# Retention and windowed-attention trunk on one core: the fifth piece's low part made by VectorE, block 0's closing norm ahead of the first rotation

## What is computed

```python
h = h + retention_layer(rmsnorm(h, ret_norm), ret_w_in, ret_w_out)
kb, vb = shared_kv(h, kv_norm, w_kv)
h = h + swa_sink_layer(rmsnorm(h, swa_norm), swa_w_in, swa_sinks, swa_w_out, kb, vb)
return rmsnorm(h, final_norm)

def retention_layer(h, w_in, w_out):
    q, k, v, g = split(h @ w_in)          # per head: q, k of 256, v, g of 512
    q, k = apply_rope(q), apply_rope(k)
    o = normalized((q k^T * decay) v + q R)    # R: the carried state
    return (o * silu(g)) @ w_out
```

## Time and profile before

| | us |
|---|---|
| median of 3 runs | 2452.99 (2448.79 to 2453.55) |
| profiled execution | 2453.43 |
| its span, first to last instruction | 2451.6 |
| block 1's heads, about | 645 to 1086 |
| TensorE busy | 2403.7 |
| VectorE busy | 1456.6 |
| ScalarE busy | 666.2 |
| GpSimd busy | 425.3 |

### The profile page before, as it was taken

How to read it: one execution, slowest core, us unless ns; L and a number is a source line. 1 busy time by engine, 2 the same in 40 slices (tenths; PEclk the granted TensorE clock), 3 DMA queues, 4 the chain that set the end, 5 groups by cost and what they waited for, 6 DMA issues and landing times.

```text
span 2451.6 us, 28645 instructions
## 1 busy us (share of the span) xinstructions
PE 2403.7 (98%) x11264; PEld 1975.1 (81%) x11264; DVE 1456.6 (59%) x2014; ACT 666.2 (27%) x1450; POOL 425.3 (17%) x310
## 2 busy tenths in 40 slices
PE   7999999999999999999999999999999999999998
PEld 6888888877778787888888888888888887888886
DVE  6554655577664655653858564655566745647384
ACT  2312312235220211122532221222352212313243
POOL 2111111221254645530010000000001100001000
PEclk9999999999999999999999999999999999999999
DMA  8667575654898888974369877775357977786433
GB/s 351 268 236 291 195 267 214 249 189 181 322 386 325 328 327 292 339 263 181 117 221 326 275 258 261 272 255 192 144 178 241 332 262 264 251 282 248 172 103 146
DMA packets 126393, 613.25 MB, mean 250 GB/s; under 512 B 8544, under 2 KB 9312, under 8 KB 104288
## 3 DMA queue, kind: packets, MB, share of 16 engines
q1 hardware_dynamic: 117424, 575.94, 65.4%
q10 hardware_dynamic: 8880, 36.18, 3.9%
HBM read 459.00 MB, written 153.09 MB: 250 GB/s over the span
## 4 chain that ended last, share of the span: by engine, by line
PE 90%; DVE 7%; issue 1%; ACT 1%; DMA 0%; POOL 0%; DVEq 0%; SPq 0%; POOLq 0%; ACTq 0%
PE ps L693 29%; PE ps L695 28%; PE ps L694 28%; PE ps L1146 2%; DVE ff L2105 1%; PE ps L1156 1%; DVE ff L1992 1%; PE ps L954 1%; DVE fr L1575 1%; PE ps L841 1%; DVE mx L2145 1%; DVE xlo L1575 0%; DVE ff L2175 0%; DMA raw<-in_stream 0%; PE ps L1086 0%
## 5 line engine op out<-in xcount | busy, mean ns | idle before, releaser
L693 PE MATMUL ps<-whl,xhi 128*128 128x512 f32 (+1 forms) x1088 | 416.8, 383 | 3.7 <-DVE xlo L1575 2.2
L695 PE MATMUL ps<-whl,xlo 128*128 128x512 f32 (+1 forms) x1088 | 411.6, 378 | 0.0
L694 PE MATMUL ps<-whl,xhi 128*128 128x512 f32 (+1 forms) x1088 | 410.5, 377 | 0.0
L693 PE MATMUL ps<-xhi,whl 128*128 128x512 f32 x768 | 303.8, 396 | 17.7 <-DVE xlo L1579 16.3
L695 PE MATMUL ps<-xhi,whl 128*128 128x512 f32 x768 | 300.4, 391 | 0.0
L694 PE MATMUL ps<-xlo,whl 128*128 128x512 f32 x768 | 299.8, 390 | 0.0
L693 PE MATMUL ps<-whl,fr 128*128 128x512 f32 x704 | 283.3, 402 | 2.3 <-DVE whl L1617 2.1
L695 PE MATMUL ps<-whl,fr 128*128 128x512 f32 x704 | 279.9, 398 | 0.0
L694 PE MATMUL ps<-whl,fr 128*128 128x512 f32 x704 | 279.6, 397 | 0.0
L693 PEld LDWEIGHTS ps<-whl,xhi 128*128 128x128 f32 x1088 | 204.9, 188 | 42.1 <-issue 3.1
L695 PEld LDWEIGHTS ps<-whl,xlo 128*128 128x128 f32 x1088 | 204.7, 188 | 38.7
(11 more groups left out here) (199 smaller groups left out, 3725.1 us busy)
## 6 DMA issues: line engine op xcount, KB each, us to landing
whl<-split_w SPq DMA_DIRECT2D x68, 2048.0 KB, 8.5
whl<-split_w SPq DMA_DIRECT2D x110, 1024.0 KB, 6.8
split_w<-whl SPq DMA_DIRECT2D x44, 2048.0 KB, 7.2
whl<-vg_w SPq DMA_DIRECT2D x64, 1024.0 KB, 6.8
raw<-in_stream SPq DMA_DIRECT2D x44, 1024.0 KB, 9.4
vg_w<-ff SPq DMA_DIRECT2D x32, 1024.0 KB, 8.8
raw<-in_stream SPq DMA_DIRECT2D x50, 512.0 KB, 9.7
whl<-comb_w SPq DMA_DIRECT2D x24, 1024.0 KB, 6.2
```

The lines of the kernel that those rows point to most:

```text
L693: pe.matmul(dst, lhs[0], rhs[0], start=start, stop=False)
L694: pe.matmul(dst, lhs[0], rhs[1], start=False, stop=False)
L695: return pe.matmul(dst, lhs[1], rhs[0], start=False, stop=stop)
```

## The change

The low part of piece 4 is taken from GpSimd (L647 falls, and `own_lo` with it) and given to VectorE as `comb_less_hi(4)`, between the output additions (0, 1) and (0, 2). That of piece 5, which stood after the addition (1, 1), comes after (1, 2). In head 0 of block 1 the closing norm of block 0 comes ahead of the first rotation; the wait for it before `comb_less_hi(0)` stays.

```diff
--- before.py
+++ after.py
@@ -625,7 +625,7 @@
                 if c == Q0:
                     h_root(Place("post", 0), 1)
             h_root(Place("post", 0), 2)
-            def comb_piece(at, j, own_lo=False):
+            def comb_piece(at, j):
 
                 pool.wait_ge(comb_raw[j % 2].sem, at(comb_raw[j % 2], 2 * (j // 2) + 2))
                 b11, b21, b12, b22 = [raw[j % 2][:, i * 512:(i + 1) * 512] for i in range(4)]
@@ -641,10 +641,6 @@
                     pool.wait_ge(comb_hi_stored.sem, Place("head", at.b, at.h - 1)(comb_hi_stored, PIECES))
                     pool.wait_ge(comb_lo_stored.sem, Place("head", at.b, at.h - 1)(comb_lo_stored, PIECES))
                 pool.tensor_scalar(stage[:, 0, :].bitcast(F32R), raw[j % 2], 1.0, 1.0, ALU.mult, ALU.mult).then_inc(comb_hi.sem, 1)
-                if own_lo:
-                    pool.wait_ge(comb_hi.sem, at(comb_hi, j + 1))
-                    pool.wait_ge(comb_lo_stored.sem, at(comb_lo_stored, j))
-                    pool.tensor_tensor(stage[:, 1, :].bitcast(F32R), raw[j % 2], stage[:, 0, :], ALU.subtract).then_inc(comb_lo.sem, 1)
 
             def x_sums_lo(b):
 
@@ -669,7 +665,7 @@
                         x_sums_lo(b)
                     o_root(at)
                     if b < FAST:
-                        comb_piece(at, 4, True)
+                        comb_piece(at, 4)
                         comb_piece(at, 5)
                     else:
                         y_sums_lo(at)
@@ -1897,6 +1893,8 @@
                         dve.tensor_tensor(dst[:, 0, :], rot[:, 0, :], sinp[:, 1, :], ALU.subtract).then_inc(rope_rot.sem, 1)
                         dve.tensor_tensor(dst[:, 1, :], rot[:, 1, :], sinp[:, 0, :], ALU.add).then_inc(rope_rot.sem, 1)
 
+                    if seam:
+                        final_norm(b - 1)
                     dve.wait_ge(ropes_scaled.sem, at(ropes_scaled, 0))
                     dve.wait_ge(w_used.sem, at(w_used, 1))
                     rope(0, rot)
@@ -1907,7 +1905,6 @@
                         split_chunk(n0 + 2)
                     if combine:
                         if seam:
-                            final_norm(b - 1)
                             dve.wait_ge(fin.sem, Place("post", b - 1)(fin, TT))
                         comb_less_hi(0)
                     dve.wait_ge(q_lo.sem, at(q_lo, 1))
@@ -2022,13 +2019,15 @@
                     if first:
                         split_chunk(n0 + 7)
                     add_to_h(0, 1)
+                    if combine:
+                        comb_less_hi(4)
                     add_to_h(0, 2)
                     add_to_h(0, 3)
                     if first:
                         split_chunk(n0 + 8)
                     for t in range(TT):
                         add_to_h(1, t)
-                        if combine and t == 1:
+                        if combine and t == 2:
                             comb_less_hi(5)
 
                 if first:
```

## The result

| | before | after |
|---|---|---|
| median of 20 runs, us | 2451.51 | 2455.20 |
| lowest to highest | 2445.97 to 2453.78 | 2453.22 to 2457.36 |
| profiled execution | 2453.43 | 2454.64 |
| its span | 2451.6 | 2452.8 |

The ratio is 1.0016 with a 95% interval of 1.0010 to 1.0022: the change makes the kernel 3.7 us slower, little, but clear of the noise. The forecast was 1.3 us faster, so it missed by 5.0 us and had the sign wrong. The new median lies inside the stated range, and the change of 3.7 us is under the 4.9 us (0.2%) that the chances went by; the direction is what was wrong. The lines of `kernel.py` are 3 or 4 lower than before for most of VectorE and TensorE, and L647 is no more.

What follows compares the result with a forecast made beforehand. TensorE, busy 98% of the span, was taken as the bound. Gains of 9.3 + 3.1 + 1.6 = 14.0 us less 12.7 us of cost left 1.3 us off the 2452.99 median: 2451.7 us, range 2442.5 to 2457.

Steps and rivals of the forecast that it cites:

- Part 1: Block 1, fourth gate product: without L647 on GpSimd, TensorE's waits there go; 9.3 us, plus 3.1 us of half clock.
- The four waits: TensorE's transposes waiting on the gate product in block 1: 8.6 us in all, longest 2.6, forecast to go whole.
- The half clock in the gain: TensorE's half-speed stretches behind the transposes' waits in heads 0 and 2 of block 1 would go: 3.1 us gained.
- The half clock in the cost: Half-speed TensorE behind two of three new waits at the starts of heads 1 to 3: 3.1 us lost.
- The three waits: TensorE waiting for the first chunk at the starts of heads 1, 2 and 3: 3.2 us each, 9.6 us lost.
- the two rows: Earlier store-to-chunk landings, mid-head 17.6 us and head's end corrected to 15.2; the forecast took 16.4 between.
- Part 2: Start of head 0, block 1: the closing norm moves into VectorE's idle time, ending TensorE's wait for the second rotation; 1.6 us gained.
- The sum: Whole kernel: 14.0 us gained less 12.7 us of cost, a net gain of 1.3 us.
- D: Head starts: slower queue, chunk 4.9 us late three times, half clock each time; 5.4 us slower, 2458.4; chance 0.12.
- B: Head starts: queue catches up in 15.1 us, chunk 1.9 us late, clock full; gain 8.3 us, 2444.7; chance 0.20.
- C: Head starts: only bytes count, group takes 13.9 us, chunk 0.7 us late; gain 11.9 us, 2441.1; chance 0.06.

Runs made afterwards that it cites:

- experiment 5: Kernel before with the closing norm moved and GpSimd's low part of piece 4 held until the fourth gate product is done: 2446.85 us, ratio 0.9987.
- experiment 8: Kernel before, unchanged, run once more for its spread and a second trace: 2450.20 us, ratio 1.0001 to before.
- experiment 1: Kernel before with only the closing norm moved ahead of the first rotation: 2449.66 us, ratio 0.9996.
- experiment 2: The change without the moved norm: 2457.22 us, ratio 1.0029 to the kernel before.
- experiment 9: The change with piece 4's low part one output addition later, behind the third: 2464.31 us, ratio 1.0056 to the kernel before.
- experiment 10: The change without the moved norm, with piece 4's low part right behind the fourth gate product: 2441.97 us, ratio 0.9964 to before.
- experiment 3: The change with VectorE making piece 4's low part right behind the fourth gate product: 2440.71 us, ratio 0.9959 to before.
- experiment 6: The change with only the load of the next head's raw piece 0 issued behind its first chunk: 2440.27 us, ratio 0.9958 to before.

## Why the prediction was wrong, point by point

- **Part 1, L647 off GpSimd: right.** The four waits are gone, the gate product takes 0.69 us, no wait took its place there. Experiment 5 showed the mechanism with GpSimd still doing the work.
- **The half clock in the gain: the largest part of the miss.** The sum booked 3.1 us for two stretches, because the one profiled execution had two. That execution was 1.9 us over the median of 20 runs; a second one had none (experiment 8). The median of three that the forecast went by was 1.5 us over that of 20 as well. The typical gain was 1 to 2 us smaller than booked, and the forecast laid the whole 14.0 on a median.
- **The half clock in the cost: mis-sized, and this turned the sign.** "I count two of three": all three waits had it, 4.8 us for 3.1. With that alone the cost is 14.4 us, over the gain of 14.0. The 2.6 us with and 1.9 us without were taken for a bound between two cases, but of the 15 waits of 1.7 to 2.8 us in four traces (before, experiments 1, 5 and 8) six brought it, one of 2.0 us among them, and nine did not, one of 2.8 us among them; all nine waits of 3.0 us and more, in the traces of the change and of experiments 2 and 9, brought it.
- **The three waits, the mechanism: right, in place, order and number.** The size: 3.2 us forecast, 3.5 measured (3.6, 3.5, 3.4 from start to start), 10.6 us for 9.6. The low part took 2.85, 2.28, 2.62 us in heads 0 to 2, for 2.9. From store to landing it was 16.6, 17.1 and 16.6 us for 16.4, so the average of the two rows was nearer than either of them (15.2 and 17.6). The store went out 13.0 to 13.6 us ahead of the head's end, for 13.2.
- **Part 2, the norm: right in the trace.** It was doubled to 8.9 us by GpSimd's L635 as allowed for, stayed hidden, and the wait of 1.5 us is gone. What it is worth in time stays open (experiment 10).
- **The sum.** 14.0 less 12.7 was a difference of two large terms, each uncertain by a few us. Measured against the first trace it is 14.0 less 15.4; against the median of before it is 12.1 less 15.4, 3.3 us slower. The 5.0 us of the miss are, by the traces: 1.0 of waits, 1.7 of the third stretch, 1.9 that the profiled execution of before was over the median of its 20 runs, and 0.6 that the one of after was under its own; together 5.2, since the account gives 1.4 where the spans differ by 1.2. That four waits would go and three come was right. Even against the execution that the sum was worked out from the change is a loss, for the cost's two terms; the gain's half clock made it a larger one.
- **The rivals.** D named the mechanism that won, the late chunk with half clock each time, and set its turning point at a delay of "3.1 with the clock lost each time". The measured delay was 3.5, past that point. B and C (a queue that catches up) were wrong: 16.6 to 17.1 us, not 15.1 or 13.9.

## What to carry to other kernels

When a wait is taken off the engine that sets the time, look at what used that wait as slack: here the DMA queue had 20.7 to 22.3 us for a group that takes about 19, and a version that takes the wait away has to give the queue room again, by an earlier store or another order of issue. Where the result of a moved operation is stored, follow that store through its queue to the next load that somebody waits for, and price it with the time from first issue to last landing of such a group elsewhere in the trace. And subtract no term that one profile shows and a second may not: with two large terms of opposite sign, look for a reordering that avoids the cost instead of forecasting the difference.

## What the runs showed of the hardware

- Half clock behind a stopped TensorE is not fixed by the wait's length alone: the same four waits of 1.7 to 2.8 us were followed by two, none and three stretches in three executions (each some 1.6 us of loss), and three waits of 2.0 to 2.5 us in experiment 5 by one; all nine waits of 3.0 us and more were followed by one. The spread of the kernel before (2447.5 to 2454.9 us in 57 executions) goes with it.
- A group of 1 + 1 + 1 + 2 MiB took 16.6 to 17.1 us from first issue to last landing from an empty queue (eight of nine times in the change and experiments 2 and 9, the ninth 18.6) and 18.7 to 19.9 behind a chunk under way (before, experiments 3 and 5). One raw MiB less ahead of the chunk was worth 2.7 to 3.3 us (experiment 6).
- VectorE and GpSimd, both with their inputs in SBUF, hold each other up by whole instructions: four norms took 8.9 us beside four differences and 4.9 alone, the differences 8.0 us beside the norms and 5.4 without them; a gate product of 0.7 us took 4.3 beside one GpSimd instruction of 4.6. The Trainium skill (SBUF — State Buffer, Who interferes with whom) describes the lock, and these rows agree with it.
